# Two of four PSUM banks of each attention-half group of the out-projection copied by VectorE instead of ScalarE

## What is computed

```python
h = rmsnorm(x, g_mix)
mq, mk, mv, mo, mi, mf, aq, ak, av = split_in(h @ w_in)
# mLSTM, 4 heads, dk = dv = 256: prompt in parallel form, each of 8 samples updates C (4, 256, 256)
num = einsum('bhts,bhsv->bhtv', w, v) + dec0 * einsum('bhvk,bhtk->bhtv', c0, q)
c1  = dec_end * c0 + einsum('bhs,bhsv,bhsk->bhvk', w_end, v, k)
o_m = rmsnorm_per_head(num / den) * g_mh * sigmoid(mo)            # 1024 columns
o_a = sliding-window grouped-query attention with sinks            # 1024 columns
y   = x + concatenate([o_m, o_a], axis=-1) @ w_out                 # the out-projection
y   = y + hierarchical_moe(rmsnorm(y))                             # 32 experts
y   = y + sigmoid(rmsnorm(y) @ w_ple_gate) * (p @ w_ple_proj);  out = rmsnorm(y)
```

## Time and profile before

| | us |
|---|---|
| median of three runs | 1835.01 |
| profiled execution, time | 1839.59 |
| profiled execution, span of the trace | 1837.9 |
| TensorE busy | 1426.3 (78% of the span) |
| VectorE busy | 267.9 (15%) |
| ScalarE busy | 295.2 (16%) |
| experts (slices 15 to 35 of 40) | DMA near 420 GB/s for most of it |

### The profile page before, as it was taken

How to read it: one execution, slowest core, us unless ns; L and a number is a source line. 1 busy time by engine, 2 the same in 40 slices (tenths; PEclk the granted TensorE clock), 3 DMA queues, 4 the chain that set the end, 5 groups by cost and what they waited for, 6 DMA issues and landing times. The chain is left out here.

```text
span 1837.9 us, 19553 instructions
## 1 busy us (share of the span) xinstructions
PE 1426.3 (78%) x7419; PEld 797.9 (43%) x7420; DVE 267.9 (15%) x684; ACT 295.2 (16%) x511; POOL 97.3 (5%) x176
## 2 busy tenths in 40 slices
PE   4999999999996576777766677767677766646996
PEld 2888888888784531111212121211121211114885
DVE  2202220056414200000000000000000000005013
ACT  3101121123201021111111111111111111114001
POOL 0000000100000011000010101010101010100000
PEclk9999998999996577676667776567766676866998
DMA  4546432478741859999999999999999999924341
GB/s 141 195 146 204 137 115 92 155 266 312 247 169 54 327 234 420 420 421 421 421 420 421 420 421 420 416 415 412 413 413 417 413 412 413 419 116 166 116 153 76
DMA packets 135230, 540.81 MB, mean 294 GB/s; under 512 B 19855, under 2 KB 41939, under 8 KB 83172
## 3 DMA queue, kind: packets, MB, share of 16 engines
q1 hardware_dynamic: 129988, 531.55, 73.6%
q0 software_dynamic: 5200, 8.67, 1.3%
HBM read 523.92 MB, written 24.62 MB: 298 GB/s over the span
## 5 line engine op out<-in xcount | busy, mean ns | idle before, releaser
L1644 PE MATMUL ps<-raw,xT_slots 128*32 128x512 f32 x1536 | 297.7, 865 | 195.0 <-DMA raw<-in_w_gate 140.4
L157 PE MATMUL ps<-hT,raw 128*128 128x264 f32 x1408 | 326.4, 393 | 0.0
L157 PEld LDWEIGHTS ps<-hT,raw 128*128 128x128 f32 x1408 | 269.5, 193 | 48.4 <-issue 2.0
L1662 PE MATMUL ps<-more,hid 128*32 128x512 f32 x1024 | 179.2, 837 | 52.5 <-DMA more<-in_w_down 29.8
L1644 PEld LDWEIGHTS ps<-raw,xT_slots 128*32 128x32 f32 x1536 | 36.6, 127 | 411.0 <-DMA raw<-in_w_gate 247.3
L1652 PEld LDWEIGHTS ps<-fold,gu 128*128 128x128 f32 x512 | 87.2, 257 | 119.7 <-ACT gu L1578 69.7
L157 PE MATMUL ps<-xT,raw 128*128 128x264 f32 x512 | 116.4, 390 | 1.0 <-PEq L276 1.0
L157 PE MATMUL ps<-mixT,raw 128*128 128x264 f32 x512 | 115.9, 386 | 1.2 <-PEq L855 1.2
L1617 DVE TENSOR_TENSOR hid<-ps,sig 128x128 f32<-128x128 f32 x32 | 9.3, 292 | 722.3 <-PE ps L1652 722.3
L1652 PE MATMUL ps<-fold,gu 128*128 128x32 f32 x512 | 95.0, 339 | 23.0 <-ACT gu L1578 23.0
L1644 PE MATMUL ps<-more,xT_slots 128*32 128x512 f32 x512 | 100.8, 915 | 11.8 <-DMA more<-in_w_up 11.8
(11 more groups left out here) (320 smaller groups left out, 839.4 us busy)
## 6 DMA issues: line engine op xcount, KB each, us to landing
raw<-in_w_gate SPq DMA_DIRECT2D x128, 1024.0 KB, 27.1
more<-in_w_down SPq DMA_DIRECT2D x128, 1024.0 KB, 27.5
raw<-in_w_up SPq DMA_DIRECT2D x64, 1024.0 KB, 28.1
more<-in_w_up SPq DMA_DIRECT2D x64, 1024.0 KB, 27.6
raw<-in_w_in SPq DMA_DIRECT2D x44, 1024.0 KB, 5.0
raw<-in_w_out SPq DMA_DIRECT2D x16, 1024.0 KB, 6.1
raw<-in_w_ple_gate SPq DMA_DIRECT2D x16, 1024.0 KB, 5.1
x_res<-in_state_mlstm_C SPq DMA_DIRECT2D x8, 1024.0 KB, 8.8
```

What stands on the lines that cost most here:

```text
L157: return nc.tensor.matmul(ps[:, j, 0:NT], core.raw[:, q % NCH, k * GW + j * P:k * GW + (j + 1) * P], xT[:, core.groups[g].k0 + c * CK + k, ...
L1644: last = nc.tensor.matmul(ps[own, (GATE, UP)[m], :], xT[:, k, i * SLOTS:(i + 1) * SLOTS], chunk(m * NCH + i)[:, k * GW:(k + 1) * GW], star ...
L1662: last = nc.tensor.matmul(ps[a * SLOTS:(a + 1) * SLOTS, YB, :], hid[:, i, :], chunk(2 * NCH + i)[:, a * GW:(a + 1) * GW], start=(i == 0), ...
```

## The change

The four attention-half groups of the out-projection get the banks "AAVV" in place of "AAAA". ScalarE's `partial(g)` now copies banks 0 and 1 only (its code is unchanged, it goes by the letters). VectorE gets a `partial(g)` of its own for banks 2 and 3, called at four places of its list: after sample_values(5), after sample_values(6), after sample_values(7), and at the end.

```diff
@@ mlstm, VectorE
+            def partial(g):
+
+                dve_banks(core, dve, first_group + 2 + g, lambda j: hT[:, 4 * g + j, :])
+
@@ mlstm, VectorE
             copy_state(2)
             weighted_values(3)
             sample_values(5)
+            partial(0)
             copy_state(3)
             sample_state(6)
             for j in range(0, 4):
                 mix(j)
             sample_values(6)
+            partial(1)
             for j in range(4, 8):
                 mix(j)
             sample_state(7)
             sample_values(7)
+            partial(2)
             dve.wait_ge(q["m_num2"], 8 * NS)
...
             link(V.tensor_tensor(mixT[:, 0:8, SEQ:NT], num[:], pT[:, MO0:MO0 + 8, SEQ:NT], ALU.mult))
+            partial(3)
@@ projection_groups
-            + groups(wo, four, KD // 2, KD, "AAAA") + groups(wo, four, 0, KD // 2, "VVVV")
+            + groups(wo, four, KD // 2, KD, "AAVV") + groups(wo, four, 0, KD // 2, "VVVV")
```

## The result

The changed kernel takes 1846.66 us (median of six runs, 1843.83 to 1852.17) against 1834.89 us (six runs): ratio 1.0065, 95% interval 1.0049 to 1.0080, or +9.0 to +14.7 us. In a second set the ratio was 1.0050 (1.0036 to 1.0065), +6.6 to +11.9 us. The medians of the first set are 11.8 us apart. The forecast was +11.0.

The account below looks back on a forecast made before the run. TensorE was taken to bound the stretch, busy 68.5 of 70.3 us. The terms 8.9 - 1.8 + 2.5 + 1.4 = +11.0 us on the 1835.0 us median gave 1846.0 us, range 1841.5 to 1849.0.

Parts of the forecast that it names:

- partial(0), the stop: In project(10), TensorE waits at bank 2 for VectorE's late copy, queued behind copy_state(2) and the store: +8.9 us.
- The wait that goes: TensorE's present stop before outer(3), waiting for weighted_values(3), disappears because outer(3) now comes later: -1.8 us.
- The clock: After the stop in project(10), TensorE comes back at 1.2 GHz: +2.5 us, bounds 0 and 3.6.
- partial(1), the second stop: In project(12), TensorE waits again at bank 2 for VectorE's copy behind sample_values(6): +1.4 us, no clock charged.
- partial(2): At project(14)'s bank 2, VectorE's copy is done with 3.2 us to spare: no stop.
- ScalarE's earlier release: decay(5) and sample_state(5) start up to 3.5 us earlier, but VectorE only waits longer for the store: worth 0.
- The rival on the other side: Not slower: partial(0) done before bank 2 is due, giving at most the 1.78 us stop, 1833.2 us; chance 0.03.
- The rival with a third stop: project(14) also waits, or the low clock lasts through outer(3): +12 to +14 us, 1848; chance 0.14.

Follow-up runs that it names:

- second trace: The changed kernel run once more with nothing altered, for another trace: 1846.75 us, ratio 1.0050 to the kernel before.
- a run at full clock: The changed kernel plus 18 extra unused matmul calls in TensorE's list ahead of the wait for bank 2 in project(10): 1845.12 us, ratio 1.0039.
- first group alone: Against the changed kernel, banks AAVV only for the first attention-half group, the other three groups AAAA: 1844.93 us, ratio 1.0044 to before.
- the experiment with the copies early: The changed kernel with partial(0) right after sample_state(5) and partial(1) ahead of mix 0 to 3: 1836.93 us, ratio 1.0004 to before.

## Why the prediction was right

The mechanism and its place held, and each term of the sum can be set beside its row.

- *partial(0), the stop.* Predicted 8.9 us; 8.74 and 8.86 in two traces. The prediction counted from the time at which bank 2 was due, 3.56 us after the start of project(10); counted so, the stop is 461.38 - 448.91 - 3.56 = 8.91 us, and 9.03 in the second trace. The route to it (store lands, copy_state(2), weighted_values(3), sample_values(5), copy: 4.00 us) was 460.90 - 456.90 = 4.00 us. Shown by moving the copy (no stop), by removing the store's wait (1.10) and by taking sample_values(5) from ahead of the copy (5.96).
- *The wait that goes.* -1.8 predicted, and the stop before outer(3) is absent in every kernel with the long stop.
- *The clock.* 2.5 us taken, with bounds 0 and 3.6. Over the 3.66 us of a run at full clock the two banks lost 1.56 us (first trace), 2.15 (second), 1.85 (first group alone: 466.97 - 461.46 = 5.51) and 1.86 (stop of 5.96 us: 465.86 - 460.34 = 5.52). This is the one mis-sized term. In the rows that I took it from the earlier trace rows the low clock went on for about 5.4 and 4.6 us of the chunk (twice what they lost); in project(10) it went on for 3.2 us in the first trace and 4.4 in the second. That less was left of project(10) than a chunk is not the reason, for by the prediction's own bound it could have lost 3.6 us. The same chunk that took 9.98 us in the trace of before took 7.39 in that of after, so a single row was a weak ground for this term. The rule of the Trainium skill, TensorE: Matmul & The Clock Gate, Part 1, that activity must release the throttle again, agrees with the windows above: the clock was at 0.50 when TensorE resumed, and at 1.00 only from 3.2 us later.
- *partial(1), the second stop.* 1.4 predicted, 1.13 in the bracket. Its cost is 1.40 us all the same: project(12) took 484.84 - 476.32 = 8.52 us to the next transposes instead of 7.12. Counted from the time at which bank 2 was due, the stop is 481.17 - 476.32 - 3.56 = 1.29 us, and banks 2 and 3 took 3.67 us instead of 3.56.
- *partial(2).* 3.2 us to spare predicted. VectorE's copies of group 2 start at 492.83 us, the first is done near 493.3 (0.43 us for one copy), and TensorE wants the bank at 485.71 + 7.2 + 3.56 = 496.5: 3.2 us.
- *ScalarE's earlier release.* Worth 0, as predicted: sample_state(5) came forward and VectorE waited 8.7 instead of 5.1 us for the store.

Together: from project(10)'s start to outer(3) 17.69 us instead of 462.24 - 453.18 = 9.06, +8.63; project(12) +1.40; outer(3) itself 0.08 shorter (1.72 to project(11) instead of 1.80): +9.95 against a sum of 11.0. The next block's first matmul, foretold near 514.2 us on the clock of the trace of before, stands at 508.85 in a trace that reached project(8) 4.27 us sooner: 513.1. The second trace gives 82.08 - 71.43 = +10.65. The measured total is +9.0 to +14.7 and +6.6 to +11.9 in its two sets, which both hold 10. That 11.0 lies so near the 11.8 us between the first medians is in part luck: the clock term was too large by 0.4 to 0.9 us, and whole executions carry differences of the clock elsewhere that no term of the sum stands for.

The rival on the other side, a gain of up to 1.8 us, needed the copy to be done ahead of the bank's slot. It did not come by the change; the experiment with the copies early shows that it would not have come then either (1.0004), because outer(3)'s stop hangs on the store and not on ScalarE. What the prediction saw only as a wait that disappears, the store behind copy_state(2), was the one thing worth changing among those tried here. The rival with a third stop did not occur in any of the traces.

The 1.8 us by which the trace of after is longer behind the stretch are mostly the clock again: the first piece of the gate projection (`ple`), far behind the change, takes

```profile
1704.45 38.79 PE L157 MATMUL ps<-xT,raw 128*128 128x264 f32 x160 [1.01 <-PEq L276]
```

against 37.56 us in the trace of before, 1.2 us more, with the clock at 0.50 for longer at its start. The rest is 0.26 us up to the experts' first matmul (L1636 in before) and 0.35 us from there to this piece. Why the clock comes back sooner in one execution than in another, in the changed kernel's own stop too (1.56 and 2.15 us), stays open; no experiment was made on it.

## What to carry to other kernels

Before work is handed to an idle engine, read that engine's list and not its busy share: VectorE was 15% busy, and the copy still came 9 us late, because the list is in order and the engine was waiting for a DMA in front of it. A PSUM bank that the busiest engine wants back belongs on a list where nothing ahead of it waits for something slower than the bank itself; ask too what that wait is for, since here a second pair of buffers was worth 2 us and the sharing nothing. When whole executions differ by chance of the clock elsewhere, compare the one stretch between two fixed instructions around the change: its 71.43 and 71.50 us told what the medians could not.

## What the runs showed of the hardware

- In the stretch from project(8) on, the granted clock fell to 0.50 in stops of TensorE of 5.96 to 8.86 us and stayed at 1.00 through stops of 1.10 to 1.97 us. Elsewhere it fell without a long stop: stops of 0.84 and 1.50 us near 136 and 138 us stand before a fall to 0.50 in the trace of before and before none in that of after, and from 290 to 298 us of the trace of before it was 0.50 while TensorE was busy throughout with matmuls of two columns. Behind a stop of 6 to 9 us the next sixteen rows of matmul took 5.4 to 6.0 us instead of 3.7.
- A short stop costs more than the idle time in its bracket: with 1.13 us idle project(12) was 1.40 us longer, in both traces of the changed kernel alike (8.52 against 7.12 us). Of the 0.27 us, 0.16 is how the rows are counted: the row of banks 0 and 1 is 3.72 us long, though at full rate bank 2 starts 3.56 us after it.
- One call of the float32 matmul with 264 columns is two rows of the trace: 18 calls were 36 rows and 8.17 us, 36 calls 72 rows and 16.18 us.
- A copy of one bank (128x264) ran in 0.43 us on VectorE and 0.39 us on ScalarE, two in a row on VectorE in 0.77 us.
